# A triangular inverse on 64x64 diagonal blocks in a DeltaNet scan (one Trainium2 core)

## The reference

```python
kk = jnp.einsum('nbhid,nbhjd->nbhij', k, k)
t_mat = jnp.where(strict, beta[..., :, None] * kk * decay, 0.0) + jnp.eye(c, dtype=F32)
...
sol = lax.linalg.triangular_solve(t_mat, rhs, left_side=True, lower=True, unit_diagonal=True)
...
def step(s, inp):
    v_new = uc - jnp.einsum('bhck,bhkv->bhcv', wc, s)
    s_next = s * gl[..., None, None] + jnp.einsum('bhck,bhcv->bhkv', kt, v_new)
```

## Time and profile before

| | us |
|---|---|
| median of 3 runs | 3073.72 (3071.84 to 3076.71) |
| profiled execution | 3081.12 |
| its span in the trace | 3079.3 |
| TensorE matmul busy | 2918.1 |
| TensorE weight load busy | 2339.2 |
| VectorE busy | 1611.7 |
| ACT busy | 1028.5 |
| scan of layer 0 in the trace | about 290 to 574 |
| scan of layer 1 in the trace | about 1950 to 2213 |

### The profile page before, as it was taken

The page is one execution under the profiler, slowest core; times in us unless marked ns, Lnnn a source line. Parts: engine busy times, 40 slices in busy tenths (PEclk is TensorE's granted clock), DMA queues, the critical chain, the costliest instruction groups (busy, mean ns, idle before and its releaser), DMA issues.

```text
span 3079.3 us, 39871 instructions
## 1 busy us (share of the span) xinstructions
PE 2918.1 (95%) x16126; PEld 2339.2 (76%) x16126; DVE 1611.7 (52%) x2653; ACT 1028.5 (33%) x1592; POOL 643.2 (21%) x262
## 2 busy tenths in 40 slices
PE   7999999999999999999999999899999999999996
PEld 1488999887788878887786448798877777887675
DVE  5546677526433433335737645667624544353745
ACT  0334443322222233224432134443332233432533
POOL 0121000121123211321123312000032242132036
PEclk9999999999999999999998999999999999999998
DMA  7421000222332112210134641000043231231034
GB/s 244 148 70 34 13 13 16 79 95 83 100 114 96 42 49 88 80 55 28 42 106 142 206 170 55 11 21 11 25 147 113 86 137 47 84 103 55 21 110 157
DMA packets 100437, 253.95 MB, mean 82 GB/s; under 512 B 10306, under 2 KB 32964, under 8 KB 99872
## 3 DMA queue, kind: packets, MB, share of 16 engines
q1 hardware_dynamic: 94314, 231.07, 22.6%
q10 hardware_dynamic: 5942, 20.33, 1.8%
HBM read 217.27 MB, written 34.08 MB: 82 GB/s over the span
## 4 chain that ended last, share of the span: by engine, by line
PE 78%; DVE 12%; ACT 3%; DMA 3%; issue 2%; POOL 1%; SPq 0%; ACTq 0%; POOLq 0%; DVEq 0%
PE ps L788 16%; PE ps L789 16%; PE ps L790 16%; PE ps L796 10%; PE ps L947 4%; PE ps L1273 3%; PE ps L906 2%; PE ps L1210 2%; PE ps L861 2%; DVE t_gcv L1906 1%; PE ps L1300 1%; DMA t_raw<-in_w_ada 1%; PE ps L890 1%; DVE t_grp L2200 1%; PE ps L1283 1%
## 5 line engine op out<-in xcount | busy, mean ns | idle before, releaser
L749 POOL TENSOR_TENSOR t_wlo<-t_raw,t_whi 128x1024 fp32r<-128x1024 f32 x248 | 618.6, 2497 | 2405.2 <-ACT t_whi L1393 2405.2
L788 PE MATMUL ps<-t_u_hi,t_whi 128*128 128x512 f32 (+1 forms) x2368 | 864.6, 365 | 11.0 <-issue 4.1
L789 PE MATMUL ps<-t_u_lo,t_whi 128*128 128x512 f32 (+1 forms) x2368 | 834.3, 352 | 0.0
L790 PE MATMUL ps<-t_u_hi,t_wlo 128*128 128x512 f32 (+1 forms) x2368 | 831.2, 351 | 0.0
L1393 ACT ACTIVATE t_whi<-t_raw 128x1024 fp32r<-128x1024 f32 x248 | 262.3, 1058 | 930.9 <-PE ps L790 726.9
L788 PEld LDWEIGHTS ps<-t_u_hi,t_whi 128*128 128x128 f32 x2368 | 450.3, 190 | 84.1 <-issue 20.1
L789 PEld LDWEIGHTS ps<-t_u_lo,t_whi 128*128 128x128 f32 x2368 | 450.2, 190 | 62.7 <-issue 6.5
L790 PEld LDWEIGHTS ps<-t_u_hi,t_wlo 128*128 128x128 f32 x2368 | 448.1, 189 | 63.6
L796 PE MATMUL ps<-t_grp 128*128 128x128 f32 x2848 | 353.6, 277 | 19.0 <-DVE t_gtok L1898 12.6
L796 PEld LDWEIGHTS ps<-t_grp 128*128 128x128 f32 x2848 | 339.0, 191 | 37.1 <-issue 20.7
L1464 ACT ACTIVATE t_grp<-ps 128x512 f32<-128x512 f32 x236 | 138.7, 597 | 304.1 <-PE ps L796 260.7
(11 more groups left out here) (249 smaller groups left out, 3734.9 us busy)
## 6 DMA issues: line engine op xcount, KB each, us to landing
t_raw<-in_w_in SPq DMA_DIRECT2D x184, 512.0 KB, 3.6
t_raw<-in_w_ada SPq DMA_DIRECT2D x48, 512.0 KB, 4.3
t_raw<-in_w_br SPq DMA_DIRECT2D x32, 512.0 KB, 3.6
t_raw<-in_w_out SPq DMA_DIRECT2D x32, 512.0 KB, 3.6
t_sg<-gate_logits SPq DMA_DIRECT2D x28, 384.0 KB, 4.2
hs<-t_hstage ACTq DMA_DIRECT2D x20, 512.0 KB, 3.7
t_hring<-hs SPq DMA_DIRECT2D x20, 512.0 KB, 6.1
t_raw<-in_fwd SPq DMA_DIRECT2D x64, 128.0 KB, 3.0
```

The lines of the kernel that those rows point to most:

```text
L749: pool.tensor_tensor(wlo[:, c % CONV, :], raw[:, s % RAW, :], whi[:, c % CONV, :].bitcast(f32), ALU.subtract).then_inc(sems["w_ready"], 1)
L788: pe.matmul(o, lh, rh, start=first, stop=False)
L789: pe.matmul(o, lh, rl, start=False, stop=False)
L790: return pe.matmul(o, ll, rh, start=False, stop=last)
```

## The change

The products Q, P and the transposed P go through a new helper, `blocks`, in place of `heads`. At levels 1 to 5 it multiplies the two diagonal 64x64 blocks of each head apart, the first from partitions 0 to 63 to PSUM partitions 0 to 63, the second from 64 to 127 to 64 to 127, both in the same bank: 8 matmuls of 64x64 a product instead of 4 of 128x128. At level 6 it multiplies one 64x64 block of each head, with inputs on one half of the partitions and output on the other: 4 matmuls. What ACT and VectorE do is unchanged; they still read 128 x 512 of the bank, and the masks drop what isn't needed.

```diff
+            def blocks(d, bank, lhs, rhs, lv, turned):
+
+                near = slice(0, 64), slice(64, P)
+                for h in range(HEADS):
+                    for k in range(2) if lv < LEVELS - 1 else (1 - d if turned else d,):
+                        m = k if lv < LEVELS - 1 else 1 - k
+                        a = slice(h * P + near[m].start, h * P + near[m].stop)
+                        b = slice(h * P + near[k].start, h * P + near[k].stop)
+                        last = pe.matmul(ps[near[m], bank, b], lhs[near[k], a], rhs[near[k], b], start=True, stop=True)
+                return last
...
-                        ln.done(heads(3 * d + 1, lambda h, c: grp[:, d, 2, c], lambda h, c: grp[:, d, 3, c]), "g_q")
+                        ln.done(blocks(d, 3 * d + 1, grp[:, d, 2, :], grp[:, d, 3, :], 1, False), "g_q")
...
-                            ln.done(heads(B + 1, lambda h, c: grp[:, d, 2, c], lambda h, c: grp[:, d, 3, c]), "g_q")
+                            ln.done(blocks(d, B + 1, grp[:, d, 2, :], grp[:, d, 3, :], lv, False), "g_q")
...
-                                ln.done(heads(B + 2, lambda h, c: grp[:, d, 4, c], lambda h, c: grp[:, d, 5, c]),
-                                        "g_p")
+                                ln.done(blocks(d, B + 2, grp[:, d, 4, :], grp[:, d, 5, :], lv, False), "g_p")
...
-                            ln.done(heads(B + 1, lambda h, c: grp[:, d, 5, c], lambda h, c: grp[:, d, 4, c]), "g_pt")
+                            ln.done(blocks(d, B + 1, grp[:, d, 5, :], grp[:, d, 4, :], lv, True), "g_pt")
```

## The result

| | before | changed |
|---|---|---|
| median of the runs | 3072.78 us (3069.36 to 3076.71, 4 runs) | 3052.16 us (3042.33 to 3055.58, 4 runs) |
| profiled execution | 3081.12 us | 3055.58 us |
| its span | 3079.3 us | 3053.8 us |
| first Q to last product, scan of layer 0 | 278.4 us | 267.3 us |
| the same, layer 1 | 257.9 us | 249.9 us |

The ratio is 0.9922, 95% interval 0.9904 to 0.994: faster by 0.8%, 20.6 us by the medians. The forecast was 3034, a gain of 40. The sign and the range held; the size was half of what I had worked out. The two scans together lost 19.1 us of trace time (536.3 to 517.2). The rest of the program, which nothing edits, took 2543.0 before and 2536.6 after.

The account below looks back on a forecast made before the run. TensorE was taken as the bound, busy 2918.1 of 3079.3 us. Products save 135 us, shape changes add 40, so TensorE loses 95; 3.3 us x 12 chunks = 40 reach the end: 3073.7 - 40 = 3034, range 3012 to 3088.

Parts of the forecast that it names:

- Parallel tiles: Products at levels 1 to 5: both diagonal tiles load and multiply at once, 0.46 us a product instead of 0.89.
- Rival 1: Tiles sharing a PSUM bank take turns: 0.90 us a product, shape changes still paid, 3088 us; chance 0.15.
- Rivals 2: Pairs can't be issued fast enough: 0.061 us a pair, 0.98 a product, 3100 us; chance 0.05 shared with the next.
- 3 (110 ns a pair on a tile): A 64x64 load doesn't run under its own tile's matmul: 0.89 us a product, 3110 us; chance 0.05 shared with Rivals 2.
- Shape changes: TensorE switching between 128 and 64 rows: 0.15 us in, 0.20 out, 0.35 a round trip, 114 of them, 40 us.
- TensorE's sum: TensorE's products fall from 278 to 143 us, 135 less, plus 40 for changes of shape: 95 us less.
- The path up to level 5: Level-4 merge starts at 412.45, not 413.93, 1.5 us gained; second level-5 X merge ends at 420.05, not 420.81.
- The path through level 6: First evacuation of level 6's K S at 421.95, not 424.57: 2.6 us a chunk gained by then.
- The second Q of level 6 waits for it: Level 6's second Q starts behind the second level-5 X merge, ending at 420.05, and so at 420.6.
- or the granted clock falls below 1.00 inside a scan, since TensorE then has gaps: Listed among the signs that the forecast is wrong, for both scans; no size or chance given.
- Rival 4: VectorE hides more than worked out: half the gain, 20 us, 3054; partial overlap or more hidden, 3056 to 3068, 0.08.
- the likeliest case: Tiles work in parallel: 3020 to 3056 us, with the forecast of 3034; chance 0.70.

Follow-up runs that it names:

- e3: The changed kernel with level 6's Q and transposed P in another PSUM bank, swapped with K S and the new values: 3037.82 us, ratio 0.9884 to the kernel before.
- e4: The changed kernel with 16 unread 64x64 products on TensorE ahead of each level-6 Q: 3039.44 us, ratio 0.9894 to the kernel before.
- e6: e3 with VectorE merging X of both directions before it transposes or merges either Y: 3011.95 us, ratio 0.9797 to the kernel before.

## Why the prediction was right, and where it was not

**Parallel tiles: right.** The step that decided the case was whether the two diagonal tiles work side by side in one bank. The pairs of a product start 29 ns apart on average, sixteen of them in 0.46 us, as forecast from the earlier trace rows; two products, 0.93 us, fill the 1.08 us of the row at 388.40 but for its own first load (0.05) and the drain behind it (0.09). Rival 1 asked for 0.90 us: refuted. The Trainium skill ("TensorEngine Tiling (Array Packing)", Gotcha 1) has it that different row tiles cannot use one PSUM bank at the same time; these rows show that they do, when they write different partitions of it, and the measurement decides. Rivals 2 (61 ns a pair) and 3 (110 ns a pair on a tile) fall with the same row: pairs on one tile are 58 ns apart, two tiles at once.

**Shape changes: right.** Into 64 rows, L790 at 389.82 streams for 0.11 us and the next start is 0.21 after it: 0.10 lost, and the uncovered load 0.05. Out of them, the drain is 0.09, and the gate step at 389.48 takes 0.22 us to the next start where its like takes 0.11. The sum is 0.35 us a round trip, the forecast's price from the earlier trace rows.

**TensorE's sum: right.** From first Q to last product TensorE is busy for 516.9 us before and 441.6 after, 75 less. The 41 us at half clock add some 20 us of busy time to the latter that the forecast did not have; without them it is 95 less, where I had 95. (The page's 81 includes 6 us outside the scans, where falls of the clock differ between the two executions as well.) Its idle time there grew from 19 to 76 us.

**The path up to level 5: right.** In the time of the earlier trace rows, the level-4 merge starts at 402.70 + 9.66 = 412.36, forecast 412.45; the second X merge of level 5 ends at 410.30 + 9.66 = 419.96, forecast 420.05. VectorE's first wait is 3.09 us, forecast 3.0. (9.66 us is the shift of the two traces.)

**The path through level 6: wrong, by 2.1 us a chunk.** The forecast has the first evacuation of K S at 421.95; it starts at 414.37 + 9.66 = 424.03. Instead of shrinking to 1.1 us, VectorE's second wait grew from 2.26 to 3.32. Two steps failed:
- "The second Q of level 6 waits for it", that is for the second merge of X. It waits for the Y merge behind it, as its bank B + 1 is the one that the transposed P of level 5 used and that VectorE reads last there. I had read off the code what data the product needs, and not what its bank needs. This is 0.76 us (e3 shows it at its place). Before, TensorE was late anyway, and the wait did not show.
- "or the granted clock falls below 1.00 inside a scan, since TensorE then has gaps". I had named it as a sign that I was wrong and given it neither a price nor a chance. It fell 12 times, 10 of them at level 6, at 1.6 us each where the interval shows one alone (changed kernel and e4). In the chunk shown, the second Q lasts 1.00 us to the next start instead of 0.58 (e3), and from the start of K S to its evacuation it is 2.17 us instead of 1.22 (e6, 406.03 to 407.25): 1.4 us.

0.76 + 1.4 is the 2.1 to rounding. From there on the forecast nearly holds: VectorE's last wait is 1.65 (2.1 forecast), and the state update comes at 434.44 where I had 432.1, so the chunk is 1.2 us shorter and not 3.5. A third cost stands outside this chunk: the forecast left every operation of VectorE at its length, and one of them took 2.67 and 2.87 us instead of 0.69 beside GpSimd, once a layer. The four intervals of layer 0 average 1.1; the first, in which no clock fall occurs and VectorE carries nothing over, is 5.0 shorter; layer 0 has 11.1 us in all and layer 1 8.0, where I had 20 each.

**Rival 4** gave the time that came out (3054, a half of the gain), by another mechanism. Its sign, a chunk in which VectorE has no wait left, did not come: VectorE waits 3.09, 3.32 and 1.65 us in the chunk shown. TensorE's matmuls waited 36.2 us (13.9 + 22.3) for VectorE's merges, in an order that suited longer products. The Trainium skill ("TensorEngine Tiling (Array Packing)", PSUM Bottleneck) says that tiling does not speed up the evacuation of PSUM, which may become the bottleneck after a 4x speed-up of TensorE. Here the products became half as long, and VectorE's part of the chain rose from 12% to 16%; but a change of VectorE's order, with no operation less, gave 26 us back (e6 against e3, some 20 of it by the order alone), so it was more the order than the amount of evacuation.

**The range.** The median of 3052 lies in the likeliest case's own range, 3020 to 3056, near its upper end. The part of the whole range above that, up to 3088, was there for rival 1, which the rows refute. The prices of the tiles and of the shape changes, from which the forecast and its bounds (3020 and 3045) were worked out, held; what pushed the time past 3045 were costs that had no bound in them: the bank, the clock, and VectorE's long operation. That the range up to 3056 still held it was luck: none of its width had been worked out for them.

## What to carry to other kernels

When an engine on the path gets faster, follow not only the data of its next instruction but also the buffer that it writes: a bank that was free long before may now be the last thing to come. Look next at the order in which the slower engine serves two streams; the step that the fast engine wants first should stand first for both streams before the rest is done for either. And gaps in TensorE's work are not free even where it only waits: price the stretch at half clock that may follow them. Last, look in the new trace for operations that take longer than their like: work of other engines falls on other moments once a loop is shorter.

## What the runs showed of the hardware

- Two 64x64 tiles of the array that differ in rows and columns load and multiply at once and write one PSUM bank, in different partitions: 29 ns a pair where one tile needs 53 to 59, and starts 7 ns apart.
- They do so only for neighbours in the list: with four heads of one half before four of the other, most starts are 53 to 59 ns apart, and two products last 1.46 and 1.95 us (the latter with a pause of 0.25) and not 1.08.
- The granted clock fell from 2.4 to 1.2 GHz 12 times inside the scans of the changed kernel, and not once in those of the kernel before. In the chunk shown it did so after TensorE had waited 0.90 and 0.87 us, and stayed down for 3.4 us. With those waits filled with work that nobody reads it no longer fell at level 6, and 5 times elsewhere. One fall at level 6 made the distance between two state updates 1.60 to 1.65 us longer.
- VectorE's operation on 128x512 (L1908) takes 0.69 us. In the eight places of five kernels where it began while GpSimd's L749 ran, it lasted 2.66 to 2.87 us, until about 0.5 us after GpSimd's end; where it began first it kept its 0.69 us. The kernel before has two places of the second kind. Why one excludes the other, no run here shows.
